# Rounding the mixer's projections into two parts: fp32r triples in place of fp32 products, with second parts in place

## What is computed

```python
p = xc @ w_in + b_in            # context, 256 tokens; the same for 512 latent tokens
hm = _mlstm_branch(q, k, v, o, ig, fg)                    # 8 heads, chunkwise scan, both directions
hh = _hgrn_branch(q, f, i, g)   # 8 heads; latents in column order, result back in row order
y = (sigmoid(gm) * (hm @ proj_m) + sigmoid(gh) * (hh @ proj_h)) @ w_out
x = x + gate * y
```

## Time and profile before

| | |
|---|---|
| median of the runs | 2985.77 us |
| the profiled execution | 2985.38 us, its span 2983.5 us |
| TensorE matmul busy | 2813.8 us, 94% of the span |
| VectorE, ScalarE, GpSimd busy | 1440.2, 942.3, 535.8 us |
| mean granted TensorE clock | 0.958 |
| moved by DMA | 280.99 MB |

### The profile page before, as it was taken

The page is one execution under the profiler, slowest core; times in us unless marked ns, Lnnn a source line. Parts: engine busy times, 40 slices in busy tenths (PEclk is TensorE's granted clock), DMA queues, the critical chain, the costliest instruction groups (busy, mean ns, idle before and its releaser), DMA issues.

```text
span 2983.5 us, 30920 instructions
## 1 busy us (share of the span) xinstructions
PE 2813.8 (94%) x12608; PEld 2118.2 (71%) x12608; DVE 1440.2 (48%) x2224; ACT 942.3 (32%) x1478; POOL 535.8 (18%) x506
## 2 busy tenths in 40 slices
PE   7999999999999997999999999999788898999998
PEld 4888888866666665855666678888576564488786
DVE  4764545434444454237611255443535876344444
ACT  4212121243444442014421244433321234252433
POOL 0101010024343341000001113311002443020211
PEclk9999999999999998999999999999986779999999
DMA  7454435131111111200112224333111112222221
GB/s 279 162 197 163 189 156 192 64 120 43 43 43 43 36 57 39 85 29 1 57 71 85 113 97 155 131 124 133 66 58 67 52 43 80 85 85 99 92 85 50
DMA packets 42910, 280.99 MB, mean 94 GB/s; under 512 B 4752, under 2 KB 4752, under 8 KB 16656
## 3 DMA queue, kind: packets, MB, share of 16 engines
q1 hardware_dynamic: 40464, 268.52, 24.2%
q10 hardware_dynamic: 2304, 10.49, 0.9%
HBM read 264.31 MB, written 14.68 MB: 94 GB/s over the span
## 4 chain that ended last, share of the span: by engine, by line
PE 82%; DVE 10%; ACT 4%; issue 1%; POOL 1%; DMA 1%; DVEq 0%; SPq 0%; POOLq 0%; ACTq 0%
PE ps L308 81%; POOL tb L2650 1%; DVE hd L1436 1%; DVE wb L2757 1%; DVE wb L2761 0%; DMA x<-in_x 0%; DVE t L890 0%; ACT hd L1375 0%; PE ps L2824 0%; ACT hd L1373 0%; DVE hd L1438 0%; DVE wl L871 0%; DVE xm L1190 0%; DVE small L2716 0%; DVE xmc L1871 0%
## 5 line engine op out<-in xcount | busy, mean ns | idle before, releaser
L308 PE MATMUL ps<-xs,wh 128*128 128x512 f32 (+1 forms) x3328 | 947.4, 371 | 16.4 <-DVE xs L895 14.2
L308 PEld LDWEIGHTS ps<-xs,wh 128*128 128x128 f32 x3328 | 603.8, 190 | 125.8 <-issue 22.4
L308 PE MATMUL ps<-xs,wl 128*128 128x512 f32 (+1 forms) x1664 | 613.1, 368 | 0.0
L871 DVE TENSOR_TENSOR wl<-w,wh 128x2048 fp32r<-128x2048 f32 (+3 forms) x130 | 283.5, 2182 | 264.1 <-ACT wh L865 264.0
L308 PE MATMUL ps<-h,wh 128*128 128x512 f32 (+1 forms) x1408 | 392.2, 365 | 8.3 <-POOL h L1087 8.3
L308 PEld LDWEIGHTS ps<-xs,wl 128*128 128x128 f32 x1664 | 315.2, 189 | 52.4
L865 ACT ACTIVATE wh<-w 128x2048 fp32r<-128x2048 f32 (+3 forms) x130 | 234.2, 1803 | 320.5 <-PE ps L308 288.7
L308 PEld LDWEIGHTS ps<-h,wh 128*128 128x128 f32 x1408 | 254.6, 190 | 51.6 <-POOL h L1087 10.0
L308 PE MATMUL ps<-h,wl 128*128 128x512 f32 (+1 forms) x704 | 256.6, 365 | 0.0
L308 PE MATMUL ps<-xp,w 128*128 128x512 f32 x512 | 234.0, 604 | 16.6 <-DVE at L1472 13.7
L1087 POOL TENSOR_TENSOR h<-t,h 128x512 fp32r<-128x512 f32 x66 | 75.7, 1151 | 778.5 <-ACT h L995 778.5
(11 more groups left out here) (401 smaller groups left out, 4062.6 us busy)
## 6 DMA issues: line engine op xcount, KB each, us to landing
w<-in_adat SPq DMA_DIRECT2D x52, 1024.0 KB, 5.2
w<-in_f1i SPq DMA_DIRECT2D x22, 1024.0 KB, 6.5
w<-in_f2i SPq DMA_DIRECT2D x22, 1024.0 KB, 4.8
w<-in_f3i SPq DMA_DIRECT2D x22, 1024.0 KB, 4.7
s_tables<-t ACTq DMA_DIRECT2D x16, 640.0 KB, 3.0
cs<-s_tables SPq DMA_DIRECT2D x16, 640.0 KB, 3.9
w<-in_ada SPq DMA_DIRECT2D x8, 1024.0 KB, 9.5
w<-in_whf SPq DMA_DIRECT2D x8, 1024.0 KB, 4.8
```

The source lines that it names most:

```text
L308: return e.matmul(out, l, r, start=st, stop=sp)
L871: e.tensor_tensor(lo[:, 0:key[2]], ap, hi[:, 0:key[2]].bitcast(F32), ALU.subtract).then_inc(*loV.of(key))
```

## The change

- All of the mixer's projections become `pe_group3`, or the new `pe_turned3` where the weights are the moving operand (v, and the context's k). New `split_hi1` and `split_lo1` round a weight tile into one of two high buffers (`HGW`, then `MGW`) and write the second part in place, into the weight's own slot (`below`, WRL lies on WR). The slot is given back when TensorE has done the tile.
- The splits are items of their own in `hgrn_items`: whqg of the next head at i=1, whv at i=6 of heads 0, 2, 4, whf of head h+2 at i=11. The v products are six in each of heads 0, 2, 4 (i=8 to 13) and none in the others.
- The mix norm writes x in two parts (`x1h`, `x1l`, column order; `c1h`, `c1l` for the context). TensorE's first four projections go k by k over four banks (`first`). The row-order copy goes to HBM (`mixed`), is read back when head 7's last projection is done, and is rounded into `x1h`, `x1l` (`rows` items, in heads 6 and 7), ahead of all the gate and q products, which all move into head 7.
- HGRN's outputs go to HBM head by head (`hgrn`) and are read back after mLSTM's k products; the merge rounds hm and hh into two parts (`branch_hi`, `branch_lo`). The head transposes of the merge come two heads behind `wo`, the hh products ahead of `wo` are gone, and the branch projections follow each gate tile.
- The diagonal product is one: VectorE adds k0 and k1 into AT first.
- The pair factors are made in place in four buffers (`EB`), where there were two of logarithms and three of factors.
- The first four HGRN tiles are loaded during FFN1, and the first two split in its last tile. Buffers of FFN2 move.

```diff
+    def split_hi1(e, w, key, high):
+        ap, there = weight(key)
+        hi = high.take(w, key)
+        w.wait_ge(*there)
+        e.activation(hi[:, 0:key[2]], ap, ACT.Copy).then_inc(*hiA.of(key))
+
+    def split_lo1(e, w, key, high):
+        ap, there = weight(key)
+        w.wait_ge(*hiA.at(key))
+        e.tensor_tensor(below(key), ap, high(key)[:, 0:key[2]].bitcast(F32), ALU.subtract).then_inc(*loV.of(key))
+
+    def pe_turned3(e, o, xh, xl, wh, wl, k, t, first, last):
+        mm(e, o, xh[:, k, t], wh[:, k, :], first, False)
+        mm(e, o, xh[:, k, t], wl[:, k, :], False, False)
+        return mm(e, o, xl[:, k, t], wh[:, k, :], False, last)
...
     def dve_mix(e, w):
...
+                e.scalar_tensor_tensor(out=columns(xms, x1l, k - 1)[1], in0=src, scalar=m1(3)[:, k - 1:k],
+                                       in1=hi.bitcast(F32), op0=ALU.add, op1=ALU.subtract).then_inc(*pmV.of(k - 1))
...
     def hgrn_items():
...
-                if i in (10, 11, 12) and h < 6:
-                    out.append(("v", h // 2 + 1, 3 * (h % 2) + i - 10))
-                out += [("early", n) for n in {(6, 10): [0], (6, 12): [1], (7, 0): [2], (7, 2): [3], (7, 5): [4],
-                                               (7, 8): [5]}.get((h, i), [])]
-                out += [("drain", n) for n in {(7, 3): [0], (7, 6): [1], (7, 9): [2], (7, 12): [3]}.get((h, i), [])]
+                if i >= 8 and h in (0, 2, 4):
+                    out.append(("v", h // 2 + 1, i - 8))
+                if i == 1 and h < 7:
+                    out.append(("split", ("whqg", h + 1, 2048)))
+                if i == 6 and h in (0, 2, 4):
+                    out.append(("split", ("whv", h // 2 + 1, 2048)))
+                if i == 11 and h < 6:
+                    out.append(("split", ("whf", h + 2, 2048)))
+                out += {(6, 11): [("split", ("wgate", 0, 1024))], (6, 13): [("rows", 0), ("rows", 1)],
+                        (7, 0): [("rows", 2), ("rows", 3)], (7, 1): [("split", ("wmq", 0, 2048))],
+                        (7, 6): [("split", ("wmq", 1, 2048))]}.get((h, i), [])
+                out += [("early", n) for n in {(7, 2): [0], (7, 3): [1], (7, 4): [2], (7, 6): [3], (7, 8): [4],
+                                               (7, 10): [5]}.get((h, i), [])]
+                out += [("drain", n) for n in {(7, 7): [0], (7, 9): [1], (7, 11): [2], (7, 13): [3]}.get((h, i), [])]
...
     def pe_hgrn(e, w):
...
-                    m = mm(e, b[:, 0:T], wv[:, k, 128 * half_:128 * half_ + 128], src[:, k, :], k == 0, k == KT - 1)
+                    m = pe_group3(e, b[:, 0:T], wh, wl, slice(128 * half_, 128 * half_ + 128), xh, xl, k, k == 0, k == KT - 1)
...
-                    for j in range(2):
-                        m = square(b, z[f"k{j}"][:, cc], z["q"][:, cc], c, j == 0, j == 1)
+                    m = square(b, AT[h % 2][:, cc], z["q"][:, cc], c)
...
     def act_mlstm(e, w):
+        for key in MLW[0:2]:
+            split_hi1(e, w, key, hg_hi)
         w.wait_ge(*endH[0].at(*endH[1:]))
...
     def dve_mlstm(e, w):
+        for key in MLW[0:2]:
+            split_lo1(e, w, key, hg_hi)
         w.wait_ge(*endH[0].at(*endH[1:]))
...
     def pe_merge(e, w):
...
-        for m_ in range(2):
-            branch(m_, 1)
...
+                if h >= 2:
+                    turn(h - 2)
...
+            for y in (1, 0):
+                branch(m_, y, wh, wl)
```

More of the change, by code:

```diff
@@ L1006, in act_ffn @@
                 split_hi(e, w, key, b2_half)
+        if F.more.get("mv"):
+            for key in HGK[0:2]:
+                split_hi1(e, w, key, hg_hi)
         act_then(e, w, F, 3)
@@ L1051, in dve_ffn @@
                         split_lo(e, w, k2_, b2_half)
+                if F.more.get("mv") and n == len(F.groups) - 1 and q == 3:
+                    for k2_ in HGK[0:2]:
+                        split_lo1(e, w, k2_, hg_hi)
                 for m in (2 * q, 2 * q + 1):
@@ L1290, in sp_hgrn @@
                 if p == 0 and h:
-                    get("whf", h)
                     get("whqg", h)
+                    if h % 2 and h < 6:
+                        get("whv", h // 2 + 1)
+                    if h < 7:
+                        get("whf", h + 1)
                 if p == 5:
                     slots.give((("whf", h, 2048),), (fP, h, "b1", "c"))
+                    if h == 7:
+                        load(e, w, ("wgate", 0, 1024), (mlP, "gate", 512))
                 if p == 9:
@@ L1298, in sp_hgrn @@
                 u, i = a
-                if i == 0 and u:
-                    get("whv", u)
                 if i == 5:
                     slots.give((("whv", u, 2048),), (vP, u, 5))
-            elif item == "early":
-                n, = a
-                if n == 0:
-                    load(e, w, ("wgate", 0, 1024), (mlP, "gate", 512))
-                elif n in (2, 4):
-                    load(e, w, ("wmq", n // 2 - 1, 2048), (mlP, "q", n - 1))
+            elif item == "split" and a[0][0] == "wgate":
+                w.wait_ge(*fP.at(7, "gs", "l"))
+                w.wait_ge(*vP.at(3, 5))
+                w.wait_ge(*rowsL.at("x"))
+                e.dma_start(XMF, xmsave).then_inc(*rowsB.of("x"))
+                for u in range(2):
+                    load(e, w, ("wmq", u, 2048), (mlP, "q", 2 * u + 1))
+            elif item == "out" and a[1] == 1:
+                h = a[0]
+                w.wait_ge(*oV.at(h, "t"))
+                e.dma_start(hhsave[:, 512 * h:512 * h + 512], OS[h % 2]).then_inc(*osL[h % 2].of(h))
+    osL = [sig(f"hg_out_saved{i}", 16) for i in range(2)]
     def factor_views(buf, hf):
@@ L1515, in square, with first @@
             return mm(e, o[:, 128 * c:128 * c + 128], l, r, st, sp)
+        def first():
+            ways = [FILL[p] for p in (1, 4, 7, 9)]
+            parts = {n: both_parts(w, (n, 0, 2048), hg_hi) for n in ("whf", "whqg")}
+            for name, half_, which, dst, part in ways:
+                banks.take(w, "fill", 0, dst, "l")
+            for k in range(KT):
+                w.wait_ge(*pmV.at(k))
+                for name, half_, which, dst, part in ways:
+                    m = pe_group3(e, banks("fill", 0, dst, "l"), *parts[name], slice(128 * half_, 128 * half_ + 128), x1h, x1l,
+                                  k, k == 0, k == KT - 1)
+                    if k == KT - 1:
+                        m.then_inc(*fP.of(0, dst, "l"))
+            for name, half_, which, dst, part in ways:
+                banks.give(("fill", 0, dst, "l"), (fA, 0, dst, "l"))
         for item, *a in HG:
```

489 lines of the change are left out of this document (286 added, 203 removed).

## The result

The changed kernel takes 2950.76 us (median, 2949.78 to 2953.52), the kernel before 2985.72 in the same comparison: ratio 0.9884, 95% interval 0.9866 to 0.9901. Forecast were 2930 us and 56 us less; it became 35. The spans of the two profiled executions, 2983.5 and 2947.9, are 35.6 apart, so the traces can be read against each other stage by stage.

A forecast was written before the change was run, and what follows sets the result against it. TensorE, busy 94% of the span, was taken as the bound; gains of 12.8 (HGRN), 20.7 (mLSTM's projections) and 22.2 (merge) summed to 56 us off 2985.38, giving 2930 us, forecast range 2915 to 2945 (0.55), wider range 2888 to 2967.

The forecast's parts named there:

- The products: All changed projections: three fp32r products for one fp32 gain 0.18 us at 512 columns, 0.07 at 256; gross 128 with the diagonal.
- HGRN's handover: Between heads: next projection waits for whf's split behind VectorE's scans; 14.8 us idle in odd heads, 4 in even.
- rival A: HGRN handovers cost nothing new, as TensorE has other work or splits come early: 2870 us; chance 0.13.
- Rival C: Inside heads, TensorE also waits for VectorE's work behind the split, 64 us lost: 2994; chance 0.07 with other slower outcomes.
- The clock: After TensorE's idle time at HGRN handovers: slow granted clock, charged 2.5 us to each handover after head 0.
- Heads 6 and 7: End of HGRN, with row copies, gate and q products, norm and mLSTM's first split: 123 us against 127.6, gain 4.
- Rival B: HGRN handovers and heads stretch as GpSimd contends with VectorE: 2950 to 2970 us; chance 0.15.
- mLSTM's projections and the scan: mLSTM: projections gain 21.7 us gross, 1 lost where the gate chain precedes the v sums; scan unchanged.
- The merge: Merge: products gain 23 us; 5.4 idle and 2.5 clock at the norm and split against 7.3 before; net 22.
- D: Products with weights moving: fp32r doesn't hold 0.36 us but takes 0.43, 29 us of gain go: 2959; chance 0.06.

The follow-up runs named there:

- early-split kernels: Changed kernel with whf split ahead of the gates: 2937.05 us; the same plus level 4's masked copy and the states' sums ahead of the gates: 2919.10 us.
- kernel with added products: Changed kernel plus 48 unread products of 512 columns on TensorE during the split wait in heads 1, 3 and 5: 2950.02 us.

## Why the prediction came out as it did

**The products.** At 256 columns the size was right (0.078 against 0.07). At 512 columns it was 0.165 instead of 0.18. The new triples take 0.694 us. These are the starts of two groups in the merge, 24 instructions apart:

```profile
1605.07 0.39 PE L308 MATMUL ps<-hmh,wh 128*128 128x512 f32 x1
...
1610.62 0.39 PE L308 MATMUL ps<-x1h,wh 128*128 128x512 f32 x1
```

5.55 us for eight, where the earlier trace rows gave 5.47. The sum had 456 x 0.18; the missing 0.015 make 7 us of it, of which 1.9 are in the merge's branches. The merge's other 192 triples also went from 0.684 to 0.694, another 1.9. Why these run slower than the same three instructions did in the trace of before is not shown by any run. The Trainium skill (FP8 and Floating Point Precision, TensorE Precision Notes) counts four passes for true fp32; the estimate from it for three passes, 0.75, is not borne out: measured is 0.694 of 0.86, 0.81. (The 16 us that the prediction gives for that estimate are for the products of 512 columns alone; those of 256 columns would add 552 x 0.0375 = 21.)

**HGRN's handover.** This was the step with most in it, and it held. Idle 14.6 us in odd heads (forecast 14.8), released by the split's line. In even heads it was 2.27 + 1.35 (forecast 4): only the second of these is for the split, the first is for the bank that level 4's masked copy frees, the wait of 2.28 that stood there before. Heads 1, 3, 5 took 59.0, 58.5, 59.3 (forecast 59.1), heads 2 and 4 64.8 and 66.2 (65.8), head 0 60.8 (60.2), and it starts at 671.0 (671.5). The early-split kernels show that it is the split's place: moved, the wait changes its name and its length. They also show what rival A would have needed, and that no order of the splits alone gives it: behind the split stands the chain of scans, GpSimd's differences, the exponential and the factors. Rival C's place (waits inside the head for factors) is thus real, but it is behind the split's wait, not added to it. The clock was charged at 2.5 us a handover. The first 24 products behind one take 7.15 to 8.50 us, and 5.55 at full clock, so it was 1.6 to 3.0, 2.1 in the mean; the triples' 0.694 made up for the difference, 0.4 us a head, and the heads' sums came out closer than their terms. The kernel with added products shows that this clock can't be saved by shortening the wait to 3.7 us. One slip is in the sum itself: the prediction's own terms for heads 0 to 5 and the start give 13.3 - 6.6 - 0.9 + 3.4 = 9.2 us, not 8.2, against the measured 9.9; in mLSTM's projections they give 224 x 0.07 + 32 x 0.18 = 21.4, not 21.7.

**Heads 6 and 7: the step that failed.** The forecast was 123 us, of them 79 behind head 7's last projection, where "HGRN's last norm 4.8 and, new, mLSTM's first split 2.2" stood between the last output and the first v product. Measured are 139.6. The step that failed is this end of the stage, a path that the prediction did not follow back to the load, together with the row copies' price.
- 8.3 us are the load: I had counted every instruction of the split and not the queue behind which its load is issued. The kernel with the loads moved shows it (139.5 to 131.2). Together with the split ahead of the norm 14.5 go, so most of the 4.8 and 2.2 was avoidable in place too.
- The row copies: VectorE was done with them 31.5 us after the last projection instead of 27.2: 4.3 us, for which the second half of the first gate product waits. Rival B's mechanism fits this place, the copies at 1.1 us beside GpSimd instead of 0.68, though no run took GpSimd's work away.
- The rest, some 4 us, is argued only: the clock. I had charged one slow start to head 7, and there are three:

```profile
1087.60:1104.70 17.10, 6.96 (x24) 5.98 (x25) 16.89 (x22) 14.18 (x17) 13.66 (x15) 0.50 0.29 120
1108.10:1114.90 6.80, 5.67 (x14) 4.51 (x15) 6.80 (x6) 0.00 (x0) 3.71 (x4) 0.50 0.00 0
1138.80:1145.60 6.80, 5.76 (x21) 5.18 (x22) 4.56 (x10) 1.82 (x3) 0.00 (x0) 0.50 0.00 0
```

**mLSTM's projections and the scan** came out as forecast (20.9 against 20.7; -0.4 against 0).

**The merge**: 16.9 instead of 22.2. Two times 1.9 are the triples, above. The other 1.5 us: the wait for the split of `wo`'s second tile is 4.56 us (forecast 5.4) and has its slow clock behind it, but what it replaced was not 7.3 us: the trace of before has a wait of 2.21 there and about 2 us of slow clock behind it. I had overrated what the old order lost.

**The rivals.** A fell by the 14.6 us waits. B is right at the row copies alone; an odd handover's scans took 1.22 and 1.58 us as in the earlier trace rows, and the heads came out at their forecast times, so it doesn't reach its 21 us. C and D fell. That the time, 2950.8, lies at rival B's lower end is chance: the 21 us missing are a load's place in a queue, the row copies, 0.015 us a product, the old merge's overrated waits and, as argued, the clock in head 7. The direction was forecast rightly; the size was overrated, 56 us for 35.

## What to carry to other kernels

When a step gets a new stage between its load and its use (here: rounding), look for everything ahead of the load in the queue that issues it; a store that waits for a late result holds up all loads behind it. An engine that waited for one instruction in another's queue had, three times in this case, a second wait just behind it: before pricing a move, read what the engine would wait for next, and whether the engine that does the moved work would only wait elsewhere. And a gain seen in place need not show in the whole (8.3 us in place were 2 in the median here, 14.5 were 7.4), so time the whole kernel several times, and know whether the trace is of a short or a long execution before explaining a stage by it.

## What was not expected of the hardware

- A wait of 3.7 us costs the same slow clock as one of 14.6 (7.12 and 7.15 us for the same products behind it, 8.48 and 8.50, 7.21 and 7.32).
- The same scan, behind the same first waits, took 136.1 us at a granted clock of 0.90, 139.4 at 0.86, and 135.5 at 0.92, as it began at 1287, 1280 and again 1287 us; begun at 1280.5 in another kernel it took 135.4 at 0.92. The changed kernel run twice had it in the same places both times (136.1, 135.8). What decides it is not shown.
- Triples of fp32r products of 512 columns step 0.684 us on one set of operands and 0.694 on another, at a granted clock of 1.00 in both.
